# Loading the recurrent head group's gate weights per head, and moving its SiLU gate projection from the load stage into the scan stage

## The reference

```python
hn = rmsnorm(h, norm_g) * (1.0 + scale) + shift     # scale, shift from silu(cond) @ ada_w + ada_b
xa, ga = hn @ w_in[:, :1024], hn @ w_in[:, 1024:2048]
xc = short_conv(xa, conv_w, conv_b)                 # centred, width 4, depthwise
r  = sigmoid(einsum('blhi,hij->blhj', xc, wa) + ba) # 8 heads of 128, for each of 2 directions
i  = sigmoid(einsum('blhi,hij->blhj', xc, wx) + bx)
log_a = -8.0 * r * softplus(-lam)
a, u = exp(log_a), sqrt(-expm1(2.0 * log_a)) * (i * xc)
h_t = a_t * h_(t-1) + u_t                           # forward and reversed; latent scans start from the context's state
y_lru = (h_forward + h_backward) * silu(ga)
```

## Time and profile before

| | us |
|---|---|
| median of 3 runs | 863.55 (863.26 to 926.7) |
| the profiled execution's own time | 863.75 |
| its span, on the slowest core (core 6) | 862.2 |
| spans of the 8 cores | 855.2 to 862.2 |
| stage 1: start to the first matmul of stage 2 | 158.34 |
| stage 2: to the first matmul of stage 3 | 158.34 to 500.45 |
| stage 3 | 500.45 to 862.2 |

### The profile page before, as it was taken

How to read it: one execution, slowest core, us unless ns; L and a number is a source line. 1 busy time by engine, 2 the same in 40 slices (tenths; PEclk the granted TensorE clock), 3 DMA queues, 4 the chain that set the end, 5 groups by cost and what they waited for, 6 DMA issues and landing times.

```text
span 862.2 us, 8726 instructions; the slowest of 8 cores (855.2 to 862.2 us)
## 1 busy us (share of the span) xinstructions
PE 534.6 (62%) x2905; PEld 290.0 (34%) x2946; DVE 505.9 (59%) x529; ACT 404.5 (47%) x454; POOL 55.1 (6%) x80
## 2 busy tenths in 40 slices
PE   0057879636625446354513127699999899999964
PEld 0045444212111112121100005375655556465621
DVE  0033321326999989998999831536474645556463
ACT  1226454266697787969798511142222314132211
POOL 1014110100000000000000020000000101010000
PEclk9999999957657666585755567799999999999988
DMA  9978910101101010100000569900220201020222
GB/s 124 225 167 189 189 38 2 13 0 12 13 0 12 0 13 0 12 0 1 0 0 0 98 139 168 168 2 25 74 89 16 92 25 74 25 74 26 74 82 89
DMA packets 27228, 50.71 MB, mean 59 GB/s; under 512 B 10800, under 2 KB 10800, under 8 KB 27184
## 3 DMA queue, kind: packets, MB, share of 16 engines
q0 software_dynamic: 18112, 22.28, 17.8%
q1 hardware_dynamic: 9072, 27.87, 9.4%
HBM read 64.04 MB, written 8.39 MB: 84 GB/s over the span
## 4 chain that ended last, share of the span: by engine, by line
PE 47%; ACT 22%; DVE 12%; DMA 10%; issue 8%; POOL 1%; ACTq 0%; DVEq 0%; POOLq 0%; SPq 0%
PE ps L586 13%; PE ps L536 11%; PE ps L306 7%; PE ps L348 6%; PE ps L508 6%; DMA adaW<-ada_w 5%; DMA Wgb<-w_in 4%; ACT tib L393 4%; ACT trb L399 3%; ACT trb L402 3%; ACT ab L396 3%; DVE xc L367 3%; ACT trb L393 2%; ACT L393 2%; PE ps L274 2%
## 5 line engine op out<-in xcount | busy, mean ns | idle before, releaser
L389 PE MATMUL ps<-xcb,Wg 128*128 128x512 bf16 (+1 forms) x157 | 61.1, 493 | 125.6 <-ACT trb L393 93.5
L348 PE MATMUL ps<-xmT,Wxs 128*128 128x512 bf16 (+1 forms) x313 | 88.9, 454 | 47.9 <-ACT xa_c L353 45.3
L508 PE MATMUL ps<-Wv,xmT 128*128 128x512 bf16 x248 | 59.9, 397 | 29.5 <-DVE Ylru L427 22.9
L593 ACT ACTIVATE xres<-xn 128x1024 f32<-128x1024 f32 x16 | 16.9, 1057 | 129.2 <-DVE xn L591 123.5
L348 PEld LDWEIGHTS ps<-xmT,Wxs 128*128 128x128 bf16 x320 | 38.7, 123 | 99.5 <-issue 80.2
L536 PE MATMUL ps<-xmT,Wu 128*128 128x256 bf16 x512 | 61.1, 280 | 16.6 <-DMA Wu<-w_in 16.6
L389 PEld LDWEIGHTS ps<-xcb,Wg 128*128 128x128 bf16 x160 | 13.4, 105 | 168.9 <-issue 165.4
L536 PE MATMUL ps<-xmT,Wgb 128*128 128x256 bf16 x512 | 58.5, 272 | 12.9 <-ACT gu L540 8.9
L586 PE MATMUL ps<-wob,Ylru 128*128 128x512 bf16 x248 | 60.6, 387 | 8.5 <-DVE st L599 8.1
L586 PE MATMUL ps<-wob,Ysgu 128*128 128x512 bf16 x249 | 60.4, 380 | 0.4
L536 PEld LDWEIGHTS ps<-xmT,Wu 128*128 128x128 bf16 x512 | 51.4, 100 | 27.3 <-issue 17.1
(11 more groups left out here) (91 smaller groups left out, 835.1 us busy)
## 6 DMA issues: line engine op xcount, KB each, us to landing
xin<-x SPq DMA_DIRECT2D x16, 512.0 KB, 7.7
xres<-x SPq DMA_DIRECT2D x16, 512.0 KB, 3.7
out<-xn SPq DMA_DIRECT2D x16, 512.0 KB, 3.0
adaW<-ada_w POOLq DMA_DIRECT2D x3, 2048.0 KB, 23.7
wob<-w_out POOLq DMA_DIRECT2D x2, 2048.0 KB, 52.1
Wga<-w_in POOLq DMA_DIRECT2D x1, 2048.0 KB, 56.2
Wxs<-w_in POOLq DMA_DIRECT2D x8, 256.0 KB, 4.3
Wv<-w_in POOLq DMA_DIRECT2D x1, 2048.0 KB, 15.5
```

The costliest lines, as they stand in the source:

```text
L348: i = e.matmul(bank(bk, 0, n), lhsT=Wxs[:, hp * 1024 + k * 128:hp * 1024 + (k + 1) * 128], rhs=xmT[:, k * TT + c0:k * TT + c1], start=(k = ...
L389: i = e.matmul(ps[:, pp * 1024 + (q0 - c0):pp * 1024 + (q1 - c0)], lhsT=Wg[:, woff:woff + 128], rhs=xcb2[:, xo + q0:xo + q1], start=True, ...
L508: i = e.matmul(bank(hf), lhsT=xmT[:, k * TT + X0 + n * 128:k * TT + X0 + (n + 1) * 128], rhs=Wv[:, k * 1024 + hf * 512:k * 1024 + (hf + 1) ...
```

## The change

It does five things. `Wga` as a whole (2 MB as bf16) is no longer loaded at the start. The 256 matmuls and 32 SiLUs of the gate projection leave stage 1, and the new `stGa(h)` issues them in stage 2, 32 matmuls and 4 SiLUs right behind each `stPa(h)`, in the same two PSUM banks 6 and 7, with its weights `Wgas` in two buffers. The gate weights `Wg` become `Wgs`, one 128x512 slice per head in two buffers (the host packs them so that a head's slice is contiguous). `late_loads` issues adaW's third slice and then `Wxs`, `Wgas`, `Wgs` for heads 0 and 1; later heads are loaded one at a time. The transposes of stage 1 alternate between banks 0 to 3 and 4 to 7, pair by pair.

```diff
-                Wgv = _es.enter_context(nc.sbuf_tensor("Wga", [128, 8 * 1024], BF16))
-                S.op('gpsimd', lambda e: e.dma_start(out=k3(Wgv[:], 1024), in_=winv[:, :, 1024:2048]), w=['Wgv'], dma=('wc', 'Wgv'))
+                def wga_load(h):
+                    S.op('gpsimd', lambda e, h=h: e.dma_start(out=k3(Wgas[:, (h % 2) * 1024:(h % 2 + 1) * 1024], 128), in_=winv[:, :, 1024 + h * 128:1024 + (h + 1) * 128]),
+                         w=[('Wgas', h % 2)], dma=('wc', 'Wgas', h % 2))
+
+                def wg_load(h):
+                    S.op('gpsimd', lambda e, h=h: e.dma_start(out=Wgs[:, (h % 2) * 512:(h % 2 + 1) * 512], in_=wg_d[:, h * 512:(h + 1) * 512]),
+                         w=[('Wgs', h % 2)], dma=('wc', 'Wgs', h % 2))
                 def late_loads():
...
-                    wxa_load(0)
-                    wxa_load(1)
+                    for h0 in range(2):
+                        wxa_load(h0)
+                        wga_load(h0)
+                        wg_load(h0)
...
+                    pb = (gi % 2) * 4
...
-                            c0 = (k // 2) * 512 + (k % 2) * 256 + tt * 128
+                            c0 = (pb + k // 2) * 512 + (k % 2) * 256 + tt * 128
...
-                        for (j, heads) in gjobs:
-                            for h in heads:
...
-                                S.op('tensor', g_mm, r=['Wgv'] + [('xmT', g2, k) for g2 in (2 * j + 1, 2 * j + 2) for k in range(8)], w=[('ps', bk)])
...
+                def stGa(h):
+                    hp = h % 2
+                    for j in range(4):
+                        bk = 6 + (ibc[0] % 2)
+                        ibc[0] += 1
...
+                                i = e.matmul(bank(bk), lhsT=Wgas[:, hp * 1024 + k * 128:hp * 1024 + (k + 1) * 128],
+                                             rhs=xmT[:, k * TT + C + j * 512:k * TT + C + (j + 1) * 512], start=(k == 0), stop=(k == 7))
...
+                        S.op('scalar', lambda e, j=j, bk=bk: e.activation(out=Ylru[:, h * T + j * 512:h * T + (j + 1) * 512], in_=bank(bk), func=AF.Silu),
+                             r=[('ps', bk)], w=[('Y', h, j)])
+                    if h + 2 < 8:
+                        wga_load(h + 2)
...
                 stPa(0)
+                stGa(0)
...
                         if pd == 1 and ph + 2 < 8:
                             stPa(ph + 2)
+                            stGa(ph + 2)
...
                     if s_ == 0:
                         stPa(1)
+                        stGa(1)
```

More of the change, by code:

```diff
@@ L161, in build_nc @@
         with contextlib.ExitStack() as _es:
-            Wg = _es.enter_context(nc.sbuf_tensor("Wg", [128, 4096], BF16))
+            Wgs = _es.enter_context(nc.sbuf_tensor("Wgs", [128, 2 * 512], BF16))
             Wxs = _es.enter_context(nc.sbuf_tensor("Wxs", [128, 2 * 1024], BF16))
+            Wgas = _es.enter_context(nc.sbuf_tensor("Wgas", [128, 2 * 1024], BF16))
             with contextlib.ExitStack() as _es:
                 adaW = _es.enter_context(nc.sbuf_tensor("adaW", [128, 8 * 3072], BF16))
-                Wgv = _es.enter_context(nc.sbuf_tensor("Wga", [128, 8 * 1024], BF16))
                 xin = _es.enter_context(nc.sbuf_tensor("xin", [128, 4 * D], F32))
@@ L289, in stC @@
                                     out=dst, in0=ps[:, c0:c0 + 256], scalar1=der[:, gmo + k:gmo + k + 1], scalar2=der[:, sho + k:sho + k + 1], op0=ALU.mult, op1=ALU.add),
-                                    r=[('ps', k // 2), gmn, shn], w=[('xmT', gi, k)])
+                                    r=[('ps', pb + k // 2), gmn, shn], w=[('xmT', gi, k)])
                         if gi == 5:
                             gx_stage()
[L293 to L297, removed]
-                        for (j, heads) in gjobs:
-                            for h in heads:
[L300 to L308, removed]
-                                S.op('tensor', g_mm, r=['Wgv'] + [('xmT', g2, k) for g2 in (2 * j + 1, 2 * j + 2) for k in range(8)], w=[('ps', bk)])
-                                S.op('scalar', lambda e, h=h, j=j, bk=bk: e.activation(out=Ylru[:, h * T + j * 512:h * T + (j + 1) * 512], in_=bank(bk), func=AF.Silu),
-                                     r=[('ps', bk)], w=[('Y', h, j)])
                 for s_ in range(18 + 2):
@@ L357, in stPa, with g_mm @@
                         wxa_load(h + 2)
+                def stGa(h):
[3 more added lines that the diff above has]
+                        ibc[0] += 1
+                        def g_mm(e, j=j, bk=bk):
+                            i = None
+                            for k in range(8):
+                                i = e.matmul(bank(bk), lhsT=Wgas[:, hp * 1024 + k * 128:hp * 1024 + (k + 1) * 128],
+                                             rhs=xmT[:, k * TT + C + j * 512:k * TT + C + (j + 1) * 512], start=(k == 0), stop=(k == 7))
+                            return i
+                        S.op('tensor', g_mm, r=[('Wgas', hp)], w=[('ps', bk)])
+                        S.op('scalar', lambda e, j=j, bk=bk: e.activation(out=Ylru[:, h * T + j * 512:h * T + (j + 1) * 512], in_=bank(bk), func=AF.Silu),
+                             r=[('ps', bk)], w=[('Y', h, j)])
+                    if h + 2 < 8:
+                        wga_load(h + 2)
                 def stPc(h, part):
@@ L378, in stG @@
                     for gate, dstb, hbo, nm in ((0, trb, Q_HBA, 'tr'), (1, tib, Q_HBX, 'ti')):
-                        woff = ((gate * 2 + d) * 8 + h) * 128
+                        woff = hp * 512 + (gate * 2 + d) * 128
                         for (c0, c1) in ((0, C), (C, C + 1024), (C + 1024, NB)):
@@ L388, in gate_mm @@
                                     q1 = min(q0 + 512, c1)
-                                    i = e.matmul(ps[:, pp * 1024 + (q0 - c0):pp * 1024 + (q1 - c0)], lhsT=Wg[:, woff:woff + 128], rhs=xcb2[:, xo + q0:xo + q1],
+                                    i = e.matmul(ps[:, pp * 1024 + (q0 - c0):pp * 1024 + (q1 - c0)], lhsT=Wgs[:, woff:woff + 128], rhs=xcb2[:, xo + q0:xo + q1],
                                                  start=True, stop=True)
                                 return i
-                            S.op('tensor', gate_mm, r=[('Wg', 0), ('Wg', 1), ('xcb', hp)], w=[('ps', 2 * pp), ('ps', 2 * pp + 1)])
+                            S.op('tensor', gate_mm, r=[('Wgs', hp), ('xcb', hp)], w=[('ps', 2 * pp), ('ps', 2 * pp + 1)])
                             S.op('scalar', lambda e, dstb=dstb, c0=c0, c1=c1, pp=pp, n=n, hbo=hbo: e.activation(
@@ L395, in stG @@
                                 r=[('ps', 2 * pp), ('ps', 2 * pp + 1), 'hba', 'hbx'], w=[(nm, si)])
+                    if d == 1 and h + 2 < 8:
+                        wg_load(h + 2)
                     S.op('scalar', lambda e: e.activation(out=ab[:, do:do + NB], in_=trb[:, do:do + NB], func=AF.Exp,
@@ L427, in stD2 @@
                         S.op('vector', lambda e: e.tensor_tensor(out=Ylru[:, h * T:(h + 1) * T], in0=ab[:, do + C:do + NB], in1=Ylru[:, h * T:(h + 1) * T], op=ALU.mult),
-                             r=[('a', si)], w=[('Yf', h)])
+                             r=[('a', si)] + [('Y', h, j) for j in range(4)], w=[('Yf', h)])
                 units = [(h, d) for h in range(8) for d in range(2)]
                 stPa(0)
+                stGa(0)
                 stPc(0, 0)
@@ L453, in build_nc @@
                         S.op('gpsimd', lambda e: e.dma_start(out=k3(late['Wv'][:], 1024), in_=winv[:, :, 3072:4096]),
-                             w=[('Wg', 0), ('Wg', 1), ('Wxs', 0), ('Wxs', 1), 'xa_c', 'xa_x'], dma=('wc', 'Wv'))
+                             w=[('Wgs', 0), ('Wgs', 1), ('Wxs', 0), ('Wxs', 1), ('Wgas', 0), ('Wgas', 1), 'xa_c', 'xa_x'], dma=('wc', 'Wv'))
             S.barrier()
```

11 lines of the change are left out of this document (4 added, 7 removed).

## The result

The changed kernel takes 881.17 us (median of 8 runs, 879.97 to 882.43), the kernel before 863.66 us on the same chip: ratio 1.0206, 95% interval 1.0193 to 1.0219. The ratio leaves out three executions of the kernel before, which took 926 to 927 us in a second, slower state of the chip. So the change is slower beyond its interval, while it stays open whether by more than 2%. The prediction was 874 us (+1.2%). The profiled execution has a span of 880.0 us, 17.8 more than before.

A forecast was written before the change was run, and what follows sets the result against it. It took DMA, then PE, to bound stage 1, and ACT's queue, waits for PE included, stage 2 from 203 us, DVE close. 863.75 - 40 + 2 + 48.6 = 874.4, forecast 874 us, range 856 to 889.

The forecast's parts named there:

- The likeliest case: Whole kernel: stage 1 saves 40 us, later heads cost 48.6, so 874 us, 1.2% slower; chance 45%.
- stage 1: Stage 1 without the gate projection: stage 2 starts at 118 instead of 158.34 us, saving 40 us (33 to 47).
- `stPa(0)` at the lower clock: Stage 2's start: PE comes from transposes, so first matmuls run at the lower clock, +2 us (0 to 4).
- per-head term: Stage 2, heads 1 to 7: ACT waits for `stGa` behind `stPa`, +6.94 us per head, 48.6 in all (26 to 96).
- the load for SiLU lies under PE's work: Stage 2, each later head: PE's matmuls cover SiLU's table load of 1.28 us, leaving the first SiLU 0.2 us late.
- Rival (2): Stage 2, ACT: both table loads stay on the path, 1.28 us more paid seven times, 883 us; chance 6%.
- Its other figure, 884 us: Stage 2: by the skill page's 2.66 us per table switch, seven further switches would make about 884 us.
- the 2 us for adaW: Stage 1's start: without `Wga` in the queue, adaW lands 2 us earlier (0 to 4.8).
- that interference: Stage 1: PE and DMA limits one us apart cost more together, and `late_loads` keeps POOL longer; 3 us added.
- rival (1): Stage 2, banks 6 and 7: PE's added work runs at the lower clock, 886 us, all cold 922; chance 12%.
- (3): Stage 1: DMA holds it, tiles pace the pairs at 8 us or more, saving 30, 884 us; chance 10%.
- case (4): Stage 1 saves 47 and PE hides more, ACT paying about 5 us per head: 852 us; chance 15%.
- case (5): Whole kernel: both sides cancel, saving 44 against 46, 864 us; chance 12%.

The follow-up runs named there:

- e1: The changed kernel with 1 instead of 8 matmuls per group of stage 2's gate projection (values differ): 853.49 us, ratio 0.9889 to the kernel before.
- e6: The changed kernel with head 7's gate projection issued later, just before unit (7, 0): 878.31 us, ratio 1.0172 to the kernel before.
- e7: The changed kernel with the gate projection of head h+1 spread over unit (h, 1), two groups before its gate matmuls: 860.94 us, ratio 0.9964.
- e2: The changed kernel with Identity in place of SiLU in the four evictions of each head: 877.16 us, ratio 1.0169 to the kernel before.
- e3: The changed kernel with the 2 MB load of Wga put back behind adaW, unused: 884.23 us, ratio 1.0242 to the kernel before.
- e4: The changed kernel with all transposes in PSUM banks 0 to 3 again: 879.69 us, ratio 1.0196 to the kernel before.
- e10: The changed kernel with gx_stage called behind the last pair instead of the sixth: 879.66 us, ratio 1.0186 to the kernel before.
- e8: The changed kernel with heads 3 to 6 in stage 1, head 7 just before unit (7, 0), one bank set: 857.81 us, ratio 0.9934.

## Why the prediction was nearly right

The likeliest case held: stage 1's gain is smaller than what `stGa` costs serially behind `stPa`. Measured against the sum, in us:

| term | forecast | measured |
|---|---|---|
| stage 1 | -40 | -37.3 |
| `stPa(0)` at the lower clock | +2 | +2.3 |
| `stGa(0)` hidden | 0 | 0 |
| heads 1 to 7 | 7 x 6.94 = 48.6 | 7 x 7.33 = 51.3 |
| rest of stages 2 and 3 | 0 | +1.5 |
| sum | +10.6 | +17.8 |

The 7.33 us were read at one head. From ACT's first square root to its last, a stretch that holds all seven, the time grew by 52.2 us on the profiled cores.

**The per-head term** was the right mechanism (e1, e6, e7) and short by 0.39 us. The step that failed in it is "the load for SiLU lies under PE's work": the load started only with the matmul's end. Rival (2) was right about that and wrong about the price: of 1.28 us only 0.39 reach the path, because later groups absorb the rest (e2 gives 3.2 us in all, give or take 2). Its other figure, 884 us, adds 9.6 us to the sum; seven whole switches at the price it names would add 18.6 and give 893. The rows show 1.28 us a load.

**Stage 1** was short by 2.7 us. Its third pair came at 61.90 (forecast 62.2), partly by luck: the 2 us for adaW do not belong to `Wga`. The slowest core before happened to be the one whose adaW came last, at 44.65, while the mean of the eight was 41.96, and with the load put back it is 41.99 (e3). The Trainium skill (DMA: Bandwidth & Descriptors, Queues, rings and completion order) says that each engine consumes one queue's descriptors in ring order; by that the term was 0, where I had taken 2 us. The means agree with it, to within the 1 us by which they scatter from kernel to kernel.

What was missing lay behind. From the fourth to the sixth pair were 16.8 us where the forecast has 13.3, because tiles of `xin` came late (at 77.98 in the rows above). From the sixth to the seventh were 15.9 where it has 13.1: `gx_stage` waited for evictions because of the second bank set and ran nearly all at the lower clock (6.56 us). I had 3 us for that interference. How it divides between clock, banks and tiles was not separated fully: e4 and e10 each move 1 to 2 us, within their intervals.

**The rest**, 1.5 us, is 0.9 in stage 2, where the 24 matmuls that follow each wait took 6.75 to 8.25 us from head to head, and 0.5 in stage 3. I leave it at scatter.

The exclusion of rival (1) held: the matmuls of `stGa` ran at 0.226 us in blocks of 16. So did the exclusion of (3) in its strong form. My case (4) needs PE's work hidden. It was not, and e7 shows that the place, not the work, made it so. That banks 6 and 7 are what makes the place bad is read from the traces alone (PE's third group of `xa` is released by ACT's eviction after 6.74 us); no run gave `stGa` banks of its own. The 864 us of case (5) are a slip: saving 44 against 46 gives 866.

## What to carry to other kernels

A matmul block moved to "an engine with idle time" is hidden only where it can run ahead of the engine that evicts it. Here it stood behind another block in the same two banks, whose last groups ACT was already waiting for, and ACT paid its full length (7.3 us for 7.2 us of matmuls). Look for the place where the evictor is busy with something else and the banks are free, and place two groups there. A stage's idle time is finite: four heads cost 2 to 2.6 us each and the next two 7 to 7.9, so try a split before moving everything.

## What the runs showed of the hardware that was not expected

In this kernel an ACT table load in front of an ACTIVATE that waits for a matmul was released with that matmul's end and not before: it started 1.11 us after ACT was free, at each of the seven heads. The load took 1.28 us wherever I looked in stage 2, with the next function right behind it. A tanh behind a SiLU needed no load, an exp behind that tanh did.

Transposes alone kept TensorE at its lower clock most of the time, and not all of it. In stage 1 without the gate projection 16 fp32 transposes took 3.65 us in most pairs, and where e6's trace has its granted clock, from 70 to 90 us, it is 0.50. Yet in e1 the 8 transposes at 113.43 us took 1.07 us (granted 0.90) and the next 8 took 1.94 (0.50). With four heads' matmuls between them (e8) the last 16 took 1.99 us, at 1.00.
